# The scan of block 1: the gate's sums of squares from VectorE to ScalarE, and the product of decays and weights directly behind the gate's product

## The reference, cut to what matters

```python
def ssd_chunked(x, dt, A, Bm, Cm):
    ...
    a_cs = jnp.cumsum(dt * A, axis=2)
    xdt = x * dt[..., None]
    seg = a_cs[:, :, :, None] - a_cs[:, :, None, :]
    decay = jnp.exp(jnp.where(lower, seg, -jnp.inf))
    cb = jnp.einsum("bclgn,bcsgn->bclsg", Cm, Bm)
    y_diag = jnp.einsum("bclsgj,bcsgjp->bclgjp", cb[..., None] * decay, xdt)
    ...
def hybrid_layer(...):
    ...
    y = bidirectional_ssd(xs, dt_f, dt_b, Bm, Cm, A_log_f, A_log_b, dt_bias_f, dt_bias_b, D)
    y = y.reshape(b, s, SSM_GROUPS, D_SSM // SSM_GROUPS)          # 2 groups of 512
    zg = jax.nn.silu(z).reshape(b, s, SSM_GROUPS, D_SSM // SSM_GROUPS)
    y_ssm = rms_norm(y * zg, ssm_norm_g.reshape(SSM_GROUPS, -1)).reshape(b, s, D_SSM)
    ...
    o = diff_attention(q, k, v, lam, slopes)
```

## Time and profile before

| what | value |
|---|---|
| median of 3 runs | 3021.56 us (3016.97 to 3022.73) |
| the profiled execution | 3017.83 us |
| its span, first to last instruction | 3016.4 us |
| busy in the span | PE 95%, DVE 74%, ACT 42%, POOL 24% |
| forward pass of the scan | about 590 to 795 us |

### The profile page before, as it was taken

One profiled execution on the slowest core, in us unless ns is written; L12 is line 12 of the kernel. 1 busy time (PEld: TensorE's weight loads), 2 busy tenths in 40 slices (PEclk: granted clock), 3 DMA queues, 4 the chain that ended last, 5 costly groups with the idle time before them and its releaser, 6 DMA issues. The chain is left out here.

```text
span 3016.4 us, 38979 instructions
## 1 busy us (share of the span) xinstructions
PE 2865.6 (95%) x14496; PEld 2271.2 (75%) x14496; DVE 2240.1 (74%) x3445; ACT 1270.9 (42%) x2298; POOL 719.9 (24%) x561
## 2 busy tenths in 40 slices
PE   7999999999899999989999999999889999999999
PEld 6788776777688878867888777745577878887887
DVE  7445744599899964855997745889886767778888
ACT  3323331477678852223477575111363322222332
POOL 1132002355211110231134234010001253332221
PEclk9999999999899999989999999999899999999999
DMA  6355324534522225432137454321002232353331
GB/s 234 108 181 171 107 80 168 191 119 140 214 83 85 99 87 201 160 99 64 56 118 222 150 160 162 110 87 60 28 14 83 90 140 99 111 211 138 112 112 56
DMA packets 222332, 370.23 MB, mean 123 GB/s; under 512 B 19066, under 2 KB 120602, under 8 KB 222146
## 3 DMA queue, kind: packets, MB, share of 16 engines
q1 hardware_dynamic: 193378, 271.00, 27.1%
q0 software_dynamic: 28768, 96.76, 8.7%
HBM read 257.30 MB, written 109.08 MB: 121 GB/s over the span
## 5 line engine op out<-in xcount | busy, mean ns | idle before, releaser
L4587 PE MATMUL banks<-b3down_r_t 128*128 128x512 f32 x1344 | 308.2, 392 | 8.2 <-DVE b3down_r_t L4619 7.5
L4587 PEld LDWEIGHTS banks<-b3down_r_t 128*128 128x128 f32 x1344 | 254.2, 189 | 62.2 <-DVE b3down_r_t L4619 7.9
L835 PE MATMUL banks<-b_hThi,b1item_hi 128*128 128x512 f32 x464 | 194.1, 418 | 1.6 <-DVE b1ln_big L529 1.3
L4340 PE MATMUL banks<-b3up_t_t,b3up_w_w 128*128 128x512 f32 x768 | 182.8, 394 | 1.2 <-DVE b3up_w_w L4297 1.2
L2658 PE MATMUL banks<-b2h_hi,b2h_whi 128*128 128x512 f32 (+1 forms) x448 | 178.6, 399 | 4.8 <-issue 2.4
L835 PE MATMUL banks<-b_hThi,b1item_lo 128*128 128x512 f32 x464 | 181.4, 391 | 0.0
L835 PE MATMUL banks<-b_hTlo,b1item_hi 128*128 128x512 f32 x464 | 181.0, 390 | 0.0
L2658 PE MATMUL banks<-b2h_lo,b2h_whi 128*128 128x512 f32 (+1 forms) x448 | 176.8, 395 | 0.0
L2658 PE MATMUL banks<-b2h_hi,b2h_wlo 128*128 128x512 f32 (+1 forms) x448 | 176.6, 394 | 0.0
L4340 PEld LDWEIGHTS banks<-b3up_t_t,b3up_w_w 128*128 128x128 f32 x768 | 143.8, 188 | 36.1 <-DVE b3up_w_w L4297 2.6
L1756 DVE CUSTOM_DVE_ANT_0 b1att_map<-banks,b1att_dist 128x1024 f32<-128x1024 f32 x128 | 151.5, 1221 | 7.9 <-PE banks L1669 5.5
(11 more groups left out here) (614 smaller groups left out, 7479.9 us busy)
## 6 DMA issues: line engine op xcount, KB each, us to landing
b1raw_w<-in_w_in SPq DMA_DIRECT2D x32, 512.0 KB, 3.6
qk_spill<-b1scan_qk SPq DMA_DIRECT2D x64, 256.0 KB, 3.2
b1out_ws<-in_w_out SPq DMA_DIRECT2D x16, 1024.0 KB, 4.9
b3upr_raw<-in_w_mlp_up SPq DMA_DIRECT2D x16, 1024.0 KB, 5.1
b3down_a_t<-act_spill SPq DMA_DIRECT2D x16, 1024.0 KB, 6.2
b3down_b_t<-in_w_mlp_down SPq DMA_DIRECT2D x16, 1024.0 KB, 8.6
b2h_stage<-in_w_in SPq DMA_DIRECT2D x30, 512.0 KB, 3.9
b1item_stage<-in_w_in SPq DMA_DIRECT2D x29, 512.0 KB, 5.3
```

Source lines behind the costliest of these rows:

```text
L835: last = K.pe.matmul(pair[:, ss], a, b, start=q % 2 == 0 and i == 0, stop=q % 2 == 1 and i == 11)
L4340: last = pe.matmul(out, y[:, 4 * half + k], z[:, k], start=c == 0, stop=c == 11)
L4587: last = pe.matmul(K.bank[b], x[:, q, cols], y[:, q], start=c == 0, stop=c == 11)
```

## The change

The two sums of squares leave DVE's `gated` and become two `Square` activations with an accumulated sum on ACT, `squares(c-1)`, which stand in round c behind exps(c,0) and ahead of decays(c,1,0); in the last round they stand ahead of the last diagonal. DVE signals a new semaphore `sc_gated` with the gate's product and goes straight on to matrix(c,0). Mean and epsilon become a function of their own, `mean(c-1)`, which waits for ACT's `sc_sq` and stands behind matrix(c,0); its signal `sc_ms` is as before. The factor 1/512 moves into the mean.

```diff
+    "sc_gated": ("dt_u", 1), "sc_sq": ("dtA", 1),
...
+    def squares(c):
+        y = m.y[c % 2]
+        a.wait_ge(*S.at("sc_gated", c + 1))
+        for gr in range(GROUPS):
+            half = slice(gr * 512, (gr + 1) * 512)
+            last = a.activation(m.zg[:, half], y[:, half], ACT.Square, accum_out=K.stat[c][:, gr:gr + 1])
+        last.then_inc(S["sc_sq"], 1)
...
             exps(c, 0)
+            if c:
+                squares(c - 1)
             decays(c, 1, 0)
...
         if c == ST:
+            squares(c - 1)
             diagonal(c - 1)
...
-        then(v.tensor_tensor(y, y, m.zg, ALU.mult))
-        for gr in range(GROUPS):
-            half = slice(gr * 512, (gr + 1) * 512)
-            vs.mark(v.tensor_tensor_reduce(m.zg[:, half], y[:, half], y[:, half], 1.0 / 512, 0.0, ALU.mult, ALU.add, s[:, gr:gr + 1]))
-        v.wait_ge(vs.sem, vs.n)
-        v.tensor_scalar(s[:, 2:4], s[:, 0:2], LN_EPS, None, ALU.add).then_inc(S["sc_ms"], 1)
+        v.tensor_tensor(y, y, m.zg, ALU.mult).then_inc(S["sc_gated"], 1)
+
+    def mean(c):
+        s = K.stat[c]
+        v.wait_ge(*S.at("sc_sq", c + 1))
+        v.tensor_scalar(s[:, 2:4], s[:, 0:2], 1.0 / 512, LN_EPS, ALU.mult, ALU.add).then_inc(S["sc_ms"], 1)
...
             matrix(c, 0)
             dve_quarters(K, QK_PLAN[ST + c][0])
+        if c:
+            mean(c - 1)
```

More of the change, by code:

```diff
@@ L1507, in gated @@
     def gated(c):
-        y, s = m.y[c % 2], K.stat[c]
+        y = m.y[c % 2]
         v.wait_ge(S["sc_yadd"], 2 * c + 2)
         v.wait_ge(*K.loads[("zg", c)])
-        then(v.tensor_tensor(y, y, m.zg, ALU.mult))
-        for gr in range(GROUPS):
-            half = slice(gr * 512, (gr + 1) * 512)
-            vs.mark(v.tensor_tensor_reduce(m.zg[:, half], y[:, half], y[:, half], 1.0 / 512, 0.0, ALU.mult, ALU.add, s[:, gr:gr + 1]))
-        v.wait_ge(vs.sem, vs.n)
-        v.tensor_scalar(s[:, 2:4], s[:, 0:2], LN_EPS, None, ALU.add).then_inc(S["sc_ms"], 1)
+        v.tensor_tensor(y, y, m.zg, ALU.mult).then_inc(S["sc_gated"], 1)
[3 more added lines that the diff above has]
+        v.tensor_scalar(s[:, 2:4], s[:, 0:2], 1.0 / 512, LN_EPS, ALU.mult, ALU.add).then_inc(S["sc_ms"], 1)
     v.wait_ge(*K.loads["eye"])
```

## The result

| kernel | median (us) | ratio to the kernel before | 95% interval |
|---|---|---|---|
| before, 13 runs | 3020.49 | 1 | |
| changed, 13 runs | 3027.01 | 1.0022 | 1.0015 to 1.0029 |

The changed kernel is slower by 6.5 us, 0.2%; the interval does not reach 1. The profiled execution has a span of 3023.5 us against 3016.4, so 7.1 more. Not all of that is the change: the first product of y and the gate starts at 616.51 instead of 613.93, and nothing ahead of it was changed. So I read distances inside the forward pass. Round n lasts from the gate's product of chunk n-1 to that of chunk n.

What follows compares the result with a forecast made beforehand. Rounds were taken as held by PE's and ACT's pace, through POOL's store, as much as by DVE. Rounds and tail +5.95 and clock +4.0 gave +10.0 on the median of 3021.56, so 3031 us; range 3018 to 3040.

Steps and rivals of the forecast that it cites:

- the likeliest case: The forecast's own case: slower, 3031 us, its own range 3027 to 3038, chance 0.48.
- Squares and decays: On ACT, squares of 1.24 us delay decays to T + 1.29 (T: gate's product's end); second half of `tri` at T + 9.04.
- `cb`, masked, store: PE's `cb` and POOL's store come 0.7 us later, masked 0.45 later; rounds 1 to 4 together +2.8.
- Still behind it, and held: End of rounds 1 to 4: product starts at 665.1, behind the store at 664.65, so it stays held; rounds grow 0.7 us.
- the second rival: End of rounds 1 to 4: the gate's product gets ahead of POOL's store, 1.23 instead of 3.29 us; -5, chance 0.14.
- The clock: PE's gap ahead of the second half of `tri` grows to 2.5 us; lower clock costs 0.8 in rounds 1 to 5, +4.0.
- Rounds 6 and 7, tail: Round 6 -0.5 (held sum of squares gone), round 7 +1.2 (PE waits for decays), tail +2.0 (squares behind outT(6)).
- The hold itself: End of a round: POOL's store sets the gate's product's end, store + 3.97 us, whenever the product comes after the store.
- +1.5 forecast for round 4: Round 4's share of the sum: 0.7 for the later store and 0.8 for PE's lower clock.

Runs made afterwards that it cites:

- e8_fill: Changed kernel with eight unused 128x512 matmuls on PE ahead of the wait for the second half of `tri` in rounds 1 to 5; 3027.0 us, 1.0020 of before.
- e2_tail: Changed kernel with only the last chunk's two sums of squares taken on DVE again; 3030.5 us, 1.0026 of the kernel before.
- e7_early_tail: Changed kernel with `scaled` ahead of the store on POOL and the last chunk's sums on DVE again; 3019.0 us, 0.9986 of the kernel before.
- e5_before_early: Kernel before with one edit on POOL: `scaled` for the next round stands ahead of the store; 3011.4 us, 0.9960 of the kernel before.
- e4_early: Changed kernel with one edit on POOL: `scaled` for the next round stands ahead of the store; 3016.0 us, 0.9989 of the kernel before.
- e6_matrix_first: Kernel before with the sums of squares kept on DVE but placed, with the mean, behind matrix(c,0); 3024.9 us, 1.0007 of the kernel before.
- e11_squares_only: Changed kernel with the squares still on ACT, but the mean ahead of matrix(c,0) on DVE; 3029.5 us, 1.0034 of the kernel before.

## Why the prediction was right, and where it was not

The forecast was slower by 10.0 us, the result is slower by 6.5, inside the range and in the likeliest case's direction. By its own steps:

- **Squares and decays: right.** 1.24 us for both and a start of the decays at T + 1.29 were forecast; 1.25 and T + 1.29 came. Second half of `tri`: T + 9.04 forecast, T + 9.03 measured.
- **`cb`, masked, store: right, the size too large.** `cb` lost its wait, masked waits for it, and the product at 671.46 started 0.46 behind the store (0.45 forecast). But the waiting added 0.25 to 0.47 us a round (e8_fill) where the sum had 0.7: in round 3, at the full clock in both kernels, `cb` came 0.58 us later against T and masked 0.22, where 0.7 and 0.45 were forecast.
- **"Still behind it, and held" in rounds 1 to 4: wrong for one of four.** I had taken the store's lead from round 2 (0.68) for all four rounds. The product at 691.02 had only 0.26 before, and the changed kernel leaves it 0.03. There the product gets ahead of `scaled`: round 4 is 2.03 us shorter. This is the second rival, in one round instead of four. e2_tail and e8_fill show it at the same place.
- **The clock: the sum right, its spread wrong.** Forecast 0.8 in each of five rounds, 4.0. It fell in two, at 2.17 and 1.39 us (e8_fill), 3.56 together; two gaps of the same length cost no clock, and 2.17 is more than the 1.8 that I had as the most for one fall. That it raises the time as a whole is not shown, since e8_fill has the changed kernel's median.
- **Rounds 6 and 7, tail: right.** -0.5, +1.2 and +2.0 forecast, -0.87, +1.46 and +2.40 measured. That all of the tail reaches the end was assumed; e2_tail and e7_early_tail don't bear it out.
- **The hold itself: right in its size, too wide in its condition.** Store plus 3.97 us was the product's end before; here 671.00 + 3.98. But "whenever the product comes after the store" does not hold: the product of 698.31 came after its store and took 1.23, and with `scaled` moved away (e5_before_early) so did all of them. What decides is when `scaled` comes. Where the prediction says that four rounds would be 2.06 us shorter without the hold, e5 has 2.02 to 2.29. The rule that I weighed against it (the Trainium skill, "SBUF — State Buffer", section "Who interferes with whom") would let the product go first whenever it issues ahead of `scaled`; the product that issues 0.50 us ahead took 3.52, the one 0.94 ahead took 1.23, so the rows do not bear out that the order of issue decides.

The part that failed is therefore the carrying of one round's margin over to its neighbours; it was worth 3.5 us (+1.5 forecast for round 4 against -2.03). The forecast of 10.0 less this 3.5 is just the 6.5 measured, but that is chance: the profile has another 2.58 us from ahead of the pass, the smaller terms missed both ways, and two experiments (e2_tail, e8_fill) moved 2 to 4 us inside the scan without showing in the median.

## What to carry to other kernels

Before moving work to an engine with idle time, look at what stands behind it in that engine's queue: a wait placed ahead of work that others need early can cost more than the work itself. Here the squares take 1.25 us, the decays behind them start 3.9 us later against the product's end, PE goes on 1.5 us later, and the 1.1 us taken from DVE save nothing. What such a wait costs hangs on what else is late: with the product no longer held (e4_early) it was 0.05 to 0.24 us in rounds 2 to 5. An engine that is busy 97% of a round may be so because another one holds its instructions; the same instruction at two durations in two rounds is the sign, and moving the holder (one instruction on POOL) gave 0.4% where moving DVE's work gave nothing. And check a margin in every round, not in one.

## What the runs showed of the hardware beside this

POOL's power on 128x2 elements takes 0.71 to 0.72 us in the changed kernel and in e6_matrix_first, where DVE reads PSUM beside it (L1577, in e6 L1568), but 1.62 to 1.64 in the kernel before, in e5_before_early and in e11_squares_only, where matrix, with both operands in SBUF, runs beside it:

```profile
648.41 0.72 POOL L1434 TENSOR_TENSOR fixed_stat<-fixed_stat,fixed_half 128x2 f32<-128x2 f32 x1 [2.74 <-DVE fixed_stat L1531]
```

```profile
646.36 1.64 POOL L1434 TENSOR_TENSOR fixed_stat<-fixed_stat,fixed_half 128x2 f32<-128x2 f32 x1 [2.74 <-DVE fixed_stat L1531]
```

The first is of the changed kernel, the second of e11. So DVE can hold POOL as POOL holds DVE. `scaled` is not the only holder on POOL either: the fading of the state (L1466, both operands in SBUF) took 2.91 us in rounds 1 to 6 of the kernel before, beside POOL's weights, and 1.21 in rounds 2 to 6 of e4_early, where the weights end before it.

And of gaps of 2.6 to 2.8 us on PE at the same place of successive rounds, two were followed by the lower clock and two were not, in the changed kernel and again in e2_tail (clock down behind the gaps of 2.83 and 2.61, full behind those of 2.62 and 2.63): the length of the gap alone does not decide. In e11_squares_only four shorter gaps, of 2.22 to 2.24 us, were all followed by it (0.93, 0.94, 0.89 and 0.94 over rounds 1, 2, 3 and 5).
